# Three edits in a two-block layer kernel: one scaling with both norms between the blocks, the output projection's norm tile by tile, and whole gate products in the first twenty heads

## The chip, the cores and the metric

The kernel runs on one core of one Trainium2 chip. The metric is device microseconds of one execution; lower is better. A core has TensorE (PE in the profile, with PEld for its weight loads), VectorE (DVE), ScalarE (ACT), GpSimd (POOL) and SyncE (SP), which here only issues DMAs.

## The reference, cut to what matters

All data are float32, 1024 tokens of width 1024. Two blocks run one after the other: a first one with differential attention, a gated delta rule and 16 experts, then this:

```python
# end of the first block                      # start of the second
x3 = rms(x, final_g)                          # h = rms(x3, norm1_g_2);  proj = h @ w_in_2
...
# sparse attention: per row a top-256 of index scores, then 8 heads of width 64 over the chosen keys
# gates = 2048 columns of proj; y_ssm and y_att from the two branches
merged = sigmoid(g_ssm) * (y_ssm @ w_proj_ssm) + sigmoid(g_att) * (y_att @ w_proj_attn)
x4 = x3 + merged @ w_out_2
h2 = rms(x4, norm2_g_2)
out = x4 + (silu(h2 @ w_ffn_gate_2) * (h2 @ w_ffn_up_2)) @ w_ffn_down_2
```

`rms(x, g)` is x times the reciprocal root of the mean of its squares (plus 1e-6), times g. So between the blocks there are two norms one after the other on the same rows.

## The kernel before, in words

The program is a list of stages. Each stage is one block with an instruction list per engine; semaphores order the engines inside it, and at its end all engines meet (the profile shows that meeting as a wait for PEq). Tokens are cut in 8 tiles (TL) of 128 rows, t = 0 to 7; KD = 8 is the number of 128-wide pieces of the width.

**Experts** (`stage_experts`). PE multiplies 16 experts (L1820), whose weights of 12 MB each stream in over SP's queue. At the stage's start SP also loads small parameters of the second block and `final_g`, spread over the 128 partitions (L1777), ahead of the weights of expert 1. POOL gathers rows (L1796) and scatters results into `x_dram` (L1801).

**Between the blocks** (`stage_between`). SP loads the eight tiles of x (L1946), then w_in chunks (L1952). POOL makes xg = x * final_g (L1968). ACT takes the sum of squares of x (L1976) and of xg (L1980). For each pair of tiles, DVE runs seven tiny instructions (L2010 to L2016) which make both norms' reciprocals, ACT takes the roots (L1984), DVE scales twice: xn = xg * r1 * norm1_g (L2023) for the projection, and x3 = xg * r0 (L2027), which SP stores to DRAM (L1955). PE transposes xn (L2042); ACT (L1988) and DVE (L2005) each copy one half out of PSUM. SP then stores hT2 to DRAM (L1958).

**Sparse attention** (`stage_sparse`). 64 heads are written out in a fixed order, n = 0 to 63: eight for each token tile i, in the tile order 0, 1, 7, 6, 5, 4, 3, 2. A head of tile i works on (i + 1) * 128 keys. DVE does `attend(n)` (L2948: mask and row maximum), ACT the exponential (L2855), PE `values(n)`: transposes of the probabilities (L2821), `logits(n + 2)` (L2797), then a piece of a gate product (L2809), then the products with V (L2831) after ACT's copy of the transposes (L2863). ACT copies each finished gate product out (L2874) and SP stores it (L2779) and loads the next gate weights (L2776) into one of two buffers. In between, DVE runs 99 units of a bitwise search for the top-256 bounds (L2897 and small ones): 33 for each of three pairs of tiles (7 and 6, 5 and 4, 3 and 2), spread evenly over heads 0 to 15, 16 to 31 and 32 to 47; the last unit of each pair builds the masks and is long. Before the first head of the next tile can finish the last tile, DVE waits for all eight products (L2956).

There are 26 gate products here. Each is eight float32 matmuls of 512 columns, which the trace records as 16. The placement is one line:

```python
if n // 2 < GN:
    gates(n // 2, n % 2)
```

So head n carries half a product, and heads 0 to 51 carry all 26.

**Output projection** (`stage_out2`). PE multiplies the eight tiles (L3071, 16 float32 matmuls or 32 records each) into four pairs of PSUM banks; DVE adds x3 from DRAM (L3103); ACT sums squares (L3089). Only after the last tile come one root for all (L3091), DVE's scaling (L3112), PE's transposes (L3079) and ACT's copies (L3095). The next stage is `stage_ffn_up`, with PE's L3165.

Of the kernel before, what the change touches and what calls it, by code (L numbers as in the profile page):

```python
# [1736 lines left out]
def stage_experts(e):  # L1737
# [12 lines left out]
    e.fgain, e.s_fgain = A.take("final_gain", D), e.keep_sem("ex_fgain")  # L1750
# [10 lines left out]
    with nc.Block() as block:  # L1761
        @block.sync
        def _(sp):
# [13 lines left out]
            sp.dma_start(e.fgain, broadcast_rows(e.in_["final_g"])).then_inc(e.s_fgain, 16)  # L1777
# [14 lines left out]
        def _(pool):  # L1792
# [125 lines left out]
    A.give(*("w_" + n for n in names), "xe", "xT", "sg", "hid", "hidT", "y", "gcol", "rows", "idxT", "gateT")  # L1918
# [3 lines left out]
def stage_between(e):  # L1922
# [4 lines left out]
    e.x3_dram = nc.dram_tensor("x3_scratch", (L, D), F32).ap()  # L1927
    x = A.take("x", TL, D)
    gain = A.take("gain1", D)
    xg = A.take("xg", TL, D)  # L1930
# [3 lines left out]
    vv = A.take("vv", 2, TL)  # L1934
    s_x = [e.sem(f"bt_xin{i}") for i in range(TL)]
    e.w_p2, e.s_wp2 = A.take("w_p2", 3, KD, 512, high=True), [e.keep_sem(f"p2_w{i}") for i in range(3)]
    s_in, s_own, s_sq, s_sg, s_xg, s_var, s_rt, s_x3, s_n, s_tr, s_ev, s_ev2 = (
        e.sem(f"bt_{n}") for n in ("in", "own", "sq", "sg", "xg", "var", "rt", "x3", "n", "tr", "ev", "ev2"))
    e.s_hst = e.keep_sem("bt_hst")
    s_st = [e.sem(f"bt_st{i}") for i in range(TL)]  # L1940
    NP = TL // 2
    with nc.Block() as block:
        @block.sync
        def _(sp):
            for t in range(TL):
# [7 lines left out]
            for t in range(TL):  # L1953
                sp.wait_ge(s_x3, t + 1)
                sp.dma_start(e.x3_dram[t * P:(t + 1) * P, :], x[:, t]).then_inc(s_st[t], 16)  # L1955
            sp.wait_ge(s_ev, TL)
            sp.wait_ge(s_ev2, TL)
            sp.dma_start(e.hT_dram, e.hT2.rearrange("p a b -> p (a b)")).then_inc(e.s_hst, 16)  # L1958
            for t in range(TL):
                sp.wait_ge(s_st[t], 16)  # L1960

        @block.gpsimd
        def _(pool):
            for t in range(TL):
                if t == 0:
                    pool.wait_ge(e.s_fgain, 16)
                pool.wait_ge(s_x[t], 16)
                nc.gpsimd.tensor_tensor(xg[:, t], x[:, t], e.fgain, ALU.mult).then_inc(s_xg, 1)  # L1968

        @block.scalar  # L1970
        def _(act):
            def squares(t):
                act.wait_ge(s_x[t], 16)
                if t:
                    act.wait_ge(s_sq, t)
                nc.scalar.activation(junk[:, 0], x[:, t], ACT.Square, accum_out=ss[:, 0, t:t + 1]).then_inc(s_sq, 1)  # L1976
                act.wait_ge(s_xg, t + 1)
                if t:
                    act.wait_ge(s_sg, t)
                nc.scalar.activation(junk[:, 1], xg[:, t], ACT.Square, accum_out=ss[:, 1, t:t + 1]).then_inc(s_sg, 1)  # L1980

            def root(i):
                act.wait_ge(s_var, i + 1)
                nc.scalar.activation(vv[:, :, 2 * i:2 * i + 2], vv[:, :, 2 * i:2 * i + 2], ACT.Sqrt).then_inc(s_rt, 1)  # L1984

            def turned(t):
                act.wait_ge(s_tr, 2 * t + 1)
                nc.scalar.activation(e.hT2[:, 0:4, t * P:(t + 1) * P], ps[:, (2 * t) % 8, :].rearrange("p (a b) -> p a b", b=P), ACT.Copy).then_inc(s_ev, 1)  # L1988

            for i in range(NP):  # L1990
                squares(2 * i)
                squares(2 * i + 1)
                root(i)
                if i:
                    turned(2 * i - 2)
                    turned(2 * i - 1)
            turned(TL - 2)
            turned(TL - 1)

        @block.vector  # L2000
        def _(dve):
            step = Steps(dve, s_own)
            def turned(t):
                dve.wait_ge(s_tr, 2 * t + 2)
                nc.vector.tensor_copy(e.hT2[:, 4:8, t * P:(t + 1) * P], ps[:, (2 * t + 1) % 8, :].rearrange("p (a b) -> p a b", b=P)).then_inc(s_ev2, 1)  # L2005

            for i in range(NP):
                c = slice(2 * i, 2 * i + 2)
                dve.wait_ge(s_sg, 2 * i + 2)
                step(nc.vector.tensor_scalar(ss[:, :, c], ss[:, :, c], 1.0 / D, None, ALU.mult))  # L2010
# [1464 lines left out]
```

## Time and profile before

| | us |
|---|---|
| median of 3 runs | 3933.43 (3932.34 to 3933.57) |
| the profiled execution, its own time | 3939.54 |
| its span, first to last instruction | 3937.7 |
| PE busy in the span | 3623.9 |
| DVE busy | 1520.3 |
| ACT busy | 759.4 |
| POOL busy | 368.3 |

Times in the rows are microseconds from the span's start, unless marked ns. A timeline row is start, duration, engine, line, operation, output and input, and count; what stands in brackets is how long the engine had sat idle before it and what ended that. PEclk is the granted TensorE clock as a share of 2.4 GHz: 1.00 is that level, 0.50 is 1.2 GHz, a value between is a mean over time at both. The ends of matmuls are modelled, so the distance between starts says more than a matmul's duration.

### The profile page before, as it was taken

The numbers are of one execution on the slowest core, as the hardware profiler recorded it, in microseconds if no ns is written. First come the engines' busy times: TensorE is split into PE (matmuls) and PEld (weight loads), VectorE is DVE, ScalarE is ACT, GpSimd is POOL, SyncE is SP. The second block draws the span as 40 slices with busy tenths as digits, with TensorE's granted clock in tenths as the row PEclk, the third lists the DMA queues.
The fourth block names the chain that finished last, engine by engine and source line by source line (L and its number), as shares of the span: only waits on it lengthen the run. The fifth ranks groups of instructions, "written<-read, shape, count | busy, mean of one in ns | idle before, by whom it ended". The sixth has DMA issues, their size and how long they took to land. (4 is left out here: it accounts for less than half of the span.)

```text
span 3937.7 us, 32752 instructions
## 1 busy us (share of the span) xinstructions
PE 3623.9 (92%) x12692; PEld 1910.6 (49%) x12692; DVE 1520.3 (39%) x2703; ACT 759.4 (19%) x1408; POOL 368.3 (9%) x347
## 2 busy tenths in 40 slices
PE   7998999987889499999987999889999899999999
PEld 3445656544765344444433664345544444444444
DVE  3526662576333400001008563978521322222420
ACT  2004451442431000000002223223220111111000
POOL 0000000014620000000001020000000122221000
PEclk8999998988989699999988999889999999999999
DMA  6400000014332598888844032112132111110300
GB/s 241 142 9 23 1 1 14 30 58 120 87 124 96 176 347 311 316 318 322 309 154 186 0 64 83 51 30 75 33 112 96 43 43 43 43 50 30 144 22 32
DMA packets 200718, 431.22 MB, mean 110 GB/s; under 512 B 71561, under 2 KB 125993, under 8 KB 187761
## 3 DMA queue, kind: packets, MB, share of 16 engines
q1 hardware_dynamic: 191154, 397.85, 29.2%
q0 software_dynamic: 8272, 29.38, 2.5%
q8 instruction: 92, 1.51, 0.2%
q10 hardware_dynamic: 1152, 2.10, 0.1%
q14 instruction: 48, 0.39, 0.0%
HBM read 380.04 MB, written 48.07 MB: 109 GB/s over the span
## 5 line engine op out<-in xcount | busy, mean ns | idle before, releaser
L1820 PE MATMUL psum<-arena 128*128 128x512 f32 x1536 | 673.1, 596 | 5.5 <-DMA arena<-in_w_gate_dram 3.1
L3165 PE MATMUL psum<-arena 128*128 128x512 f32 x1232 | 531.5, 594 | 5.7 <-DVE arena L3223 4.1
L1820 PEld LDWEIGHTS psum<-arena 128*128 128x128 f32 x1536 | 290.4, 191 | 365.5 <-issue 362.5
L3165 PEld LDWEIGHTS psum<-arena 128*128 128x128 f32 x1232 | 234.4, 191 | 302.2 <-issue 294.5
L3319 PE MATMUL psum<-arena 128*128 128x512 f32 x528 | 228.6, 595 | 3.6 <-PEq L3138 3.6
L2809 PE MATMUL psum<-arena 128*128 128x512 f32 x416 | 201.7, 629 | 0.1
L742 PE MATMUL psum<-arena 128*128 128x512 f32 (+1 forms) x512 | 198.2, 543 | 1.1 <-PEq L456 1.1
L2897 DVE TENSOR_SCALAR_CACHE_REDUCE arena<-arena 128x1024 f32<-128x1024 f32 (+2 forms) x192 | 173.7, 943 | 1.9
L477 PE MATMUL psum<-arena 64*128 64x512 f32 (+1 forms) x384 | 156.1, 551 | 11.1 <-ACT arena L531 10.2
L3319 PEld LDWEIGHTS psum<-arena 128*128 128x128 f32 x528 | 100.3, 190 | 132.0 <-issue 131.8
L2113 PE MATMUL psum<-arena 128*128 128x512 f32 (+1 forms) x384 | 162.1, 582 | 0.0
L3234 DVE TENSOR_TENSOR arena<-arena,psum 128x512 f32<-128x512 f32 x44 | 30.3, 688 | 305.7 <-PE psum L3165 305.7
L742 PEld LDWEIGHTS psum<-arena 128*128 128x128 f32 x512 | 97.1, 191 | 96.3 <-issue 93.0
L1911 DVE SCALAR_TENSOR_TENSOR arena<-psum,arena 128x1024 f32<-128x1024 f32 x16 | 20.6, 1285 | 309.8 <-PE psum L1820 309.8
L3154 POOL TENSOR_TENSOR arena<-arena 128x512 f32<-128x512 f32 x22 | 28.7, 1304 | 1153.1 <-issue 783.3
L350 PE MATMUL psum<-arena 128*128 128x512 f32 (+1 forms) x320 | 127.8, 555 | 1.9 <-PEq L154 1.9
L2809 PEld LDWEIGHTS psum<-arena 128*128 128x128 f32 x416 | 77.9, 197 | 103.8 <-issue 102.3
L2113 PEld LDWEIGHTS psum<-arena 128*128 128x128 f32 x384 | 88.8, 233 | 68.5 <-issue 55.6
L1577 PE MATMUL psum<-arena 128*128 128x512 f32 x256 | 114.3, 607 | 1.8 <-PEq L1438 1.8
L1897 DVE TENSOR_TENSOR arena<-arena,psum 128x1024 f32<-128x1024 f32 x16 | 19.6, 1223 | 242.5 <-PE psum L1820 242.5
L3008 PE MATMUL psum<-arena 128*128 128x512 f32 x256 | 112.2, 601 | 0.9 <-PEq L2771 0.9
L3071 PE MATMUL psum<-arena 128*128 128x512 f32 x256 | 110.1, 592 | 2.4 <-PEq L2984 2.4
(514 smaller groups left out, 4674.2 us busy)
## 6 DMA issues: line engine op xcount, KB each, us to landing
arena<-in_w_gate_dram SPq DMA_DIRECT2D x32, 2048.0 KB, 7.4
arena<-in_w_up_dram SPq DMA_DIRECT2D x32, 2048.0 KB, 9.1
arena<-in_w_down_dram SPq DMA_DIRECT2D x32, 2048.0 KB, 8.0
arena<-in_w_mod_dram SPq DMA_DIRECT2D x12, 2048.0 KB, 9.5
arena<-gd_rows SPq DMA_DIRECT2D x56, 256.0 KB, 4.3
arena<-in_w_in_dram SPq DMA_DIRECT2D x22, 512.0 KB, 4.3
arena<-in_w_ffn_gate_dram SPq DMA_DIRECT2D x11, 1024.0 KB, 5.4
arena<-in_w_ffn_up_dram SPq DMA_DIRECT2D x11, 1024.0 KB, 5.4
```

The lines of the kernel that those rows point to most:

```text
L350: ins = nc.tensor.matmul(e.ps[:, i % 4, 0:n], w[:, c % 2, k, m * P:(m + 1) * P], e.hT[:, k, s:s + n], start=(k == 0), stop=(k == KD - 1))
L477: ins = nc.tensor.matmul(ps[:, 3 * m + j, 0:n], e.qT[64 * m:64 * m + 64, h, t * P:(t + 1) * P], e.kT[64 * m:64 * m + 64, h, c:c + n], star ...
L742: ins = nc.tensor.matmul(e.ps[:, i % 4, 0:n], w[:, (m // 2) % 2, k, (m % 2) * P:(m % 2 + 1) * P], e.hT[:, k, s:s + n], start=(k == 0), sto ...
L1577: ins = nc.tensor.matmul(ps[:, 2 * (t % 2) + j, :], cat(k)[:, t * P:(t + 1) * P], w[:, k, j * 512:(j + 1) * 512], start=(k == 0), stop=(k ...
L1820: ins = nc.tensor.matmul(ps[:, banks + j, :], lhs[:, k], W[n][:, h, k % 4, j * 512:(j + 1) * 512], start=(k == 0), stop=(k == KD - 1))
L2113: ins = nc.tensor.matmul(ps[:, BANK(i), 0:n], lhs, w[:, (c + 2) % 3, k, 0:n], start=(k == 0), stop=(k == KD - 1))
L2809: ins = nc.tensor.matmul(ps[:, 7, :], wg[:, c % 2, k], hT[:, k, n * 512:(n + 1) * 512], start=(k == 0), stop=(k == KD - 1))
L2897: nc.vector.tensor_scalar((rank, equal)[j][:, 0:(i + 1) * P], B(i), bound[:, j:j + 1], 0.0, ALU.is_ge, ALU.add, accum_out=count[:, j:j + 1 ...
L3008: ins = nc.tensor.matmul(ps[:, 2 * (i % 4) + g, :], wp[:, g, k, m * P:(m + 1) * P], y[:, k, n * 512:(n + 1) * 512], start=(k == 0), stop=( ...
L3071: ins = nc.tensor.matmul(ps[:, 2 * (t % 4) + j, :], e.merged[:, k, t * P:(t + 1) * P], w[:, k, j * 512:(j + 1) * 512], start=(k == 0), sto ...
L3165: ins = nc.tensor.matmul(out(q), left[:, k], right[:, k], start=first and k == 0, stop=last and k == 3, skip_group_check=not first)
L3319: ins = nc.tensor.matmul(ps[:, bank + t, :], left(c)[:, tok(t)], right(c), start=first and c == 0, stop=c == KC - 1, skip_group_check=not ...
```

## The change

1. **Between the blocks.** The POOL multiplication, x3 and its eight stores and the loading of `norm1_g_2` in this stage go. The experts' stage loads `final_g` and `norm1_g_2` into two free rows (`e.rows`), and POOL makes their product and the square of `final_g` there. In the stage itself ACT squares x once per tile and keeps the squares, DVE multiplies them by final_g squared and sums (`tensor_tensor_reduce`), and each tile is scaled once, by a factor with both norms. ACT does all sixteen copies out of PSUM. The first norm's factor is kept (`e.r3`).
2. **Output projection.** It loads x instead of x3 and makes x3 by one DVE instruction per tile. Root, scaling and transposes follow each tile: PE transposes tile t - 2 after it has multiplied tile t. The products use two pairs of PSUM banks instead of four.
3. **Gate products.** Heads 0 to 19 carry one whole product each, heads 20 to 31 a half each, and later heads none.

```diff
 stage_experts, SP:
-            sp.dma_start(e.fgain, broadcast_rows(e.in_["final_g"])).then_inc(e.s_fgain, 16)
+            sp.dma_start(e.rows[:, 1], broadcast_rows(e.in_["final_g"])).then_inc(s_fgain, 16)
+            sp.dma_start(e.rows[:, 2], broadcast_rows(e.in_["norm1_g_2"][0])).then_inc(s_fgain, 16)
 stage_experts, POOL, after gather(0) and gather(1):
+            pool.wait_ge(s_fgain, 32)
+            nc.gpsimd.tensor_tensor(e.rows[:, 2], e.rows[:, 2], e.rows[:, 1], ALU.mult).then_inc(e.s_gains, 1)
+            pool.wait_ge(e.s_gains, 1)
+            nc.gpsimd.tensor_tensor(e.rows[:, 1], e.rows[:, 1], e.rows[:, 1], ALU.mult).then_inc(e.s_gains, 1)
 stage_between, ACT:
+                nc.scalar.activation(x2[:, t % 4], x[:, t], ACT.Square, scale=D ** -0.5, accum_out=ss[:, 0, t:t + 1]).then_inc(s_sq, 1)
...
+            for t in range(4):
+                squares(t)
+            root(0)
+            squares(4)
+            turned(0)
+            turned(1)
+            root(1)
+            squares(5)
+            squares(6)
+            turned(2)
+            turned(3)
+            root(2)
+            squares(7)
+            turned(4)
+            turned(5)
+            root(3)
+            turned(6)
+            turned(7)
 stage_between, DVE:
+                nc.vector.tensor_tensor_reduce(out=junk[:, t % 2], in0=x2[:, t % 4], in1=gain_sq, scale=1.0, scalar=0.0, op0=ALU.mult, op1=ALU.add,
+                                               accum_out=ss[:, 1, t:t + 1]).then_inc(s_s1, 1)
...
+                nc.vector.scalar_tensor_tensor(out=xn[:, t % 2], in0=x[:, t], scalar=rr[:, 1, t:t + 1], in1=gains, op0=ALU.mult, op1=ALU.mult).then_inc(s_n, 1)
...
+            sum_with_gain(0)
+            sum_with_gain(1)
+            for i in range(TL // 2):
+                spread(i)
+                if i < TL // 2 - 1:
+                    sum_with_gain(2 * i + 2)
+                scaled(2 * i)
+                scaled(2 * i + 1)
+                if i < TL // 2 - 1:
+                    sum_with_gain(2 * i + 3)
 stage_sparse:
+    EARLY = 2 * HEADS + 4
+    halves = lambda n: ((n, 0), (n, 1)) if n < EARLY else (divmod(n + EARLY, 2),)
+    ready = lambda n: n if n < EARLY else (n + EARLY) // 2 if (n + EARLY) % 2 else None
...
-                if n // 2 < GN:
-                    gates(n // 2, n % 2)
+                for q, half in halves(n):
+                    if q < GN:
+                        gates(q, half)
...
-                if n >= 2 and n % 2 == 0 and n // 2 <= GN:
-                    gates((n - 2) // 2)
+                if n >= 1 and ready(n - 1) is not None and ready(n - 1) < GN:
+                    gates(ready(n - 1))
 stage_out2, PE:
+                ins.then_inc(s_mm, 1)
+                if t >= 2:
+                    turn(t - 2)
+            turn(TL - 2)
+            turn(TL - 1)
 stage_out2, ACT:
+            for t in range(TL):
+                squares(t)
+                root(t)
+                if t >= 2:
+                    turned(t - 2)
+            turned(TL - 2)
+            turned(TL - 1)
 stage_out2, DVE:
+                nc.vector.scalar_tensor_tensor(out=e.x4[:, t], in0=xr[:, t % 2], scalar=e.r3[:, t:t + 1], in1=g[:, 0], op0=ALU.mult, op1=ALU.mult).then_inc(s_x3, 1)
...
+            for t in range(TL):
+                residual(t)
+                spread(t)
+                modulated(t)
```

## Rows read from the trace of the kernel before

**Rows 1.** The page: busy time, share of the span and instructions of each engine.

```profile
PE 3623.9 (92%) x12692; PEld 1910.6 (49%) x12692; DVE 1520.3 (39%) x2703; ACT 759.4 (19%) x1408; POOL 368.3 (9%) x347
```

**Rows 2.** The timeline between the blocks, 2062 to 2112 us.

```profile
2066.34 18.47 POOL L1968 TENSOR_TENSOR arena<-arena 128x1024 f32<-128x1024 f32 x8 [11.35 <-DMA arena<-x_scratch]
...
2080.45 2.05 DVE L2016 TENSOR_TENSOR arena<-arena 128x2 f32<-128x2 f32 x1
...
2085.94 3.68 PE L2042 MATMUL psum<-arena 128*128 128x128 f32 x16 [34.74 <-DVE arena L2023]
...
2089.53 0.17 DVE L2016 TENSOR_TENSOR arena<-arena 128x2 f32<-128x2 f32 x1
...
2089.97 2.48 DVE L2023 SCALAR_TENSOR_TENSOR arena<-arena 128x1024 f32<-128x1024 f32 x2 [0.28 <-ACT arena L1984]
...
2111.12 1.30 PE L2142 MATMUL psum<-arena 128*128 128x128 f32 x8 [2.68 <-PEq L1942]
```

**Rows 3.** The timeline at the experts' start, around 1383 us.

```profile
1383.39 8.81 PE L1820 MATMUL psum<-arena 128*128 128x512 f32 x16 [3.09 <-DMA arena<-in_w_gate_dram]
```

**Rows 4.** The timeline at the end of the output projection, 3107 to 3125 us.

```profile
3107.13 1.22 DVE L3103 TENSOR_TENSOR arena<-arena,psum 128x1024 f32<-128x1024 f32 x1 [12.51 <-PE psum L3071]
3108.39 1.06 ACT L3089 ACTIVATE arena<-arena 128x1024 f32<-128x1024 f32 x1 [12.58 <-DVE arena L3103]
...
3118.40 0.86 PEld L3079 LDWEIGHTS psum<-arena 128*128 128x128 f32 x8 [0.34 <-DVE arena L3112]
...
3124.23 3.67 PE L3165 MATMUL psum<-arena 128*128 128x512 f32 x8 [0.99 <-PEq L3045]
```

**Rows 5.** DVE's timeline: `attend` of heads 0, 15, 16, 32, 47, 48, 53, 54, 55.

```profile
2466.96 0.29 DVE L2948 CUSTOM_DVE_ANT_0 arena<-psum,arena 128x128 f32<-128x128 f32 x1 [0.46 <-PE psum L2797]
...
2559.03 0.42 DVE L2948 CUSTOM_DVE_ANT_0 arena<-psum,arena 128x256 f32<-128x256 f32 x1
...
2580.08 1.22 DVE L2948 CUSTOM_DVE_ANT_0 arena<-psum,arena 128x1024 f32<-128x1024 f32 x1
...
2714.06 0.95 DVE L2948 CUSTOM_DVE_ANT_0 arena<-psum,arena 128x768 f32<-128x768 f32 x1
...
2809.98 0.83 DVE L2948 CUSTOM_DVE_ANT_0 arena<-psum,arena 128x640 f32<-128x640 f32 x1 [2.18 <-PE psum L2797]
...
2822.90 0.69 DVE L2948 CUSTOM_DVE_ANT_0 arena<-psum,arena 128x512 f32<-128x512 f32 x1
...
2847.97 0.69 DVE L2948 CUSTOM_DVE_ANT_0 arena<-psum,arena 128x512 f32<-128x512 f32 x1 [5.08 <-PE psum L2797]
2853.93 0.69 DVE L2948 CUSTOM_DVE_ANT_0 arena<-psum,arena 128x512 f32<-128x512 f32 x1 [5.08 <-PE psum L2797]
2856.46 0.69 DVE L2948 CUSTOM_DVE_ANT_0 arena<-psum,arena 128x512 f32<-128x512 f32 x1 [1.65 <-PE psum L2797]
```

**Rows 6.** PE's timeline: transposes of heads 6, 16, 20, 21; the next stage's first product.

```profile
2504.22 0.33 PE L2821 MATMUL psum<-arena 128*128 128x128 f32 x1 [1.42 <-ACT arena L2855]
...
2582.82 1.97 PE L2821 MATMUL psum<-arena 128*128 128x128 f32 x8 [16.06 <-ACT arena L2855]
...
2621.87 1.04 PE L2821 MATMUL psum<-arena 128*128 128x128 f32 x8
...
2630.02 1.04 PE L2821 MATMUL psum<-arena 128*128 128x128 f32 x8
...
2882.41 4.48 PE L3008 MATMUL psum<-arena 128*128 128x512 f32 x5 [0.94 <-PEq L2771]
```

**Rows 7.** Windows: busy us of PE, PEld, DVE, ACT, POOL, then PEclk, DMA share, GB/s.

```profile
2582.80:2593.10 10.30, 10.28 (x18) 4.82 (x19) 9.85 (x28) 2.73 (x4) 0.00 (x0) 0.50 0.28 76
...
2714.10:2822.90 108.80, 107.23 (x459) 63.30 (x458) 76.92 (x262) 32.35 (x58) 0.00 (x0) 1.00 0.19 59
...
2853.80:2876.00 22.20, 21.15 (x124) 14.15 (x123) 8.14 (x32) 11.38 (x30) 0.00 (x0) 1.00 0.00 1
```

**Rows 8.** The gate weights' loads (L2776) by source line.

```profile
DMA to landing us min/median/max: 4.0/4.2/5.4
```

More of the change, by code:

```diff
@@ L1917, in _ @@
                 output(i, False)
-    A.give(*("w_" + n for n in names), "xe", "xT", "sg", "hid", "hidT", "y", "gcol", "rows", "idxT", "gateT")
+    A.give(*("w_" + n for n in names), "xe", "xT", "sg", "hid", "hidT", "y", "gcol", "idxT", "gateT")
 def stage_between(e):
@@ L1926, in stage_between @@
     e.hT_dram = nc.dram_tensor("hT_scratch", (P, KD * L), F32).ap()
-    e.x3_dram = nc.dram_tensor("x3_scratch", (L, D), F32).ap()
     x = A.take("x", TL, D)
-    gain = A.take("gain1", D)
-    xg = A.take("xg", TL, D)
+    x2 = A.take("x2", 4, D)
     xn = A.take("xn", 2, D)
@@ L1973, in squares @@
                 act.wait_ge(s_x[t], 16)
[L1974 to L1980, printed above, removed]
+                if t >= 4:
+                    act.wait_ge(s_s1, t - 3)
+                nc.scalar.activation(x2[:, t % 4], x[:, t], ACT.Square, scale=D ** -0.5, accum_out=ss[:, 0, t:t + 1]).then_inc(s_sq, 1)
             def root(i):
                 act.wait_ge(s_var, i + 1)
-                nc.scalar.activation(vv[:, :, 2 * i:2 * i + 2], vv[:, :, 2 * i:2 * i + 2], ACT.Sqrt).then_inc(s_rt, 1)
+                nc.scalar.activation(rr[:, :, 2 * i:2 * i + 2], vv[:, :, 2 * i:2 * i + 2], ACT.Sqrt).then_inc(s_rt, 1)
             def turned(t):
[L1987 to L1998, printed above, removed]
+                for j in range(2):
+                    act.wait_ge(s_tr, 2 * t + j + 1)
+                    nc.scalar.activation(e.hT2[:, 4 * j:4 * j + 4, t * P:(t + 1) * P],
+                                         ps[:, (2 * t + j) % 8, :].rearrange("p (a b) -> p a b", b=P), ACT.Copy).then_inc(s_ev, 1)
+            for t in range(4):
[16 more added lines that the diff above has]
+            turned(7)
         @block.vector
@@ L2002, in _, with sum_with_gain, spread @@
             step = Steps(dve, s_own)
[L2003 to L2007, printed above, removed]
+            def sum_with_gain(t):
+                dve.wait_ge(s_sq, t + 1)
+                if t >= 2:
+                    dve.wait_ge(s_s1, t - 1)
+                nc.vector.tensor_tensor_reduce(out=junk[:, t % 2], in0=x2[:, t % 4], in1=gain_sq, scale=1.0, scalar=0.0, op0=ALU.mult, op1=ALU.add,
+                                               accum_out=ss[:, 1, t:t + 1]).then_inc(s_s1, 1)
+            def spread(i):
                 c = slice(2 * i, 2 * i + 2)
-                dve.wait_ge(s_sg, 2 * i + 2)
-                step(nc.vector.tensor_scalar(ss[:, :, c], ss[:, :, c], 1.0 / D, None, ALU.mult))
+                dve.wait_ge(s_s1, 2 * i + 2)
                 step(nc.vector.tensor_scalar(vv[:, 0, c], ss[:, 0, c], EPS, None, ALU.add))
@@ L2044, in _ @@
                         ins.then_inc(s_tr, 1)
-    A.give("x", "xn", "gain1", "final_gain", "junk", "ss", "xg", "vv")
+    A.give("x", "xn", "x2", "junk", "ss", "vv", "rows")
 TWO_PI = 2 * np.pi
@@ L3037, in stage_out2 @@
     xr = A.take("x_ring", 2, D)
-    g = A.take("gain", D)
+    g = A.take("gain", 2, D)
     h = A.take("h", 2, D)
@@ L3042, in stage_out2 @@
     s_x = [e.sem(f"o2_xin{i}") for i in range(2)]
-    s_g, s_mm, s_x4, s_sq, s_var, s_rt, s_own, s_h, s_tr, s_ev = (e.sem(f"o2_{n}") for n in ("g", "mm", "x4", "sq", "var", "rt", "own", "h", "tr", "ev"))
+    s_g = [e.sem(f"o2_g{i}") for i in range(2)]
+    s_mm, s_x3, s_x4, s_sq, s_var, s_rt, s_own, s_h, s_tr, s_ev = (e.sem(f"o2_{n}") for n in ("mm", "x3", "x4", "sq", "var", "rt", "own", "h", "tr", "ev"))
     two = lambda v: v.rearrange("p (a n) -> p a n", a=2)
```

117 lines of the change are left out of this document (49 added, 68 removed).

## The prediction

> **What bounds the kernel now.** I read the page first: PE is busy 92% of the span [rows 1], so only two things shorten the run: stretches in which PE waits, and PE work at the low clock. I then read the timeline of the three places that the change touches, and windows for the granted clock.
>
> Between the blocks PE sits 34.74 us without work before its first transposes [rows 2]. x starts to land at 2066.3; DVE's first tiny instructions, two elements per row, take up to 2.05 us while POOL multiplies (2066.34 to 2084.8), and 0.17 us once it is done [rows 2]. That convoy, not DMA, holds the stage from 2070 on.
>
> In the output projection PE works without a gap to about 3107.1, then the norm of all tiles runs alone: the next stage's PE starts at 3124.2 [rows 4], a tail of 17.1 us.
>
> In sparse attention the bound changes. Heads 0 to 15 go at DVE's pace, (2559.03 - 2466.96) / 15 = 6.14 us [rows 5], PE idle about 1.3 us in each [rows 6]; the mask unit of head 15 then holds everything from 2559.03 to 2580.08, and PE idles 16.06 us and comes back at 1.2 GHz: eight transposes take 1.97 us where they take 1.04 later [rows 6], and the window to 2593.1 is granted 0.50 [rows 7]. From head 20 on PE is the bound: 8.15 us a head [rows 6], and 107.2 of 108.8 us busy in heads 32 to 47, where DVE has 76.9 us of work [rows 7].
>
> **Part 1, experts.** One more broadcast row of 0.5 MB is in front of expert 1's weights on SP, and PE waits 3.09 us for these already [rows 3]. A load of 0.5 MB costs SP's queue between nothing and one such load; the bounds are 0 and 3 us, and I take 1.6. The two POOL multiplications (18.47 / 8 = 2.3 us each [rows 2]) delay the gather for expert 2, which is needed two experts' first halves later: nothing.
>
> **Part 2, between the blocks.** What is left on DVE: eight new reductions, eight scalings of 2.48 / 2 = 1.24 us, four groups of six tiny steps at 0.20 us from start to start, so 1.2 us each [rows 2]. The reduction is not in this stage's trace; the nearest row is the same kind of instruction in `attend`, 1.22 us for 1024 elements [rows 5], and its accumulator read makes 1.31. Bounds: 1.1 and, were both inputs in SBUF dearer, 1.6; I take 1.31. In order: x0 lands at 2066.2, ACT's square is done at 2067.4; two reductions to 2070.1; six steps to 2071.3. ACT has by then four squares (tiles land some 1.4 us apart) to 2071.7 and loads its root table until 2073.0, so the first scaling starts at 2073.25. From there DVE has 8 x 1.24 + 5 x 1.31 + 3 x 1.2 = 20.1 us, with 0.6 us of wait for the last root, to 2094.0. The last tile's eight transposes take 3.68 / 2 = 1.85 us at the low clock [rows 2], ACT's last copy 0.6: 2096.5. All copies now being ACT's costs nothing: 16 x 0.6 + 8 x 1.15 us of work in 30. The end meeting waits for the issue of SP's store of hT2, some 0.9 us: 2097.4 against 2111.1 [rows 2]. **-13.7**, with bounds -10 (dear reductions, late x) and -15. The x3 stores that go were hidden.
>
> **Part 3, output projection.** The transposes of tiles 0 to 4 go into the stream of products, 0.86 us each [rows 4]: +4.3. After the last product: the addition to +1.3, squares to +2.4 [rows 4], two small steps and a root (its table has been in since the first tile) to +3.2, the scaling to +4.5. ACT copies tiles 5, 6 and 7 in order and is through at +6.9; the next stage starts at +7.1 instead of +17.1. x3's instruction on DVE runs under the 13.7 us of a tile's products, and so does the wait for one of only two PSUM pairs. The last store of x4 leaves at +1.3 and the next stage needs it at +7. 4.3 + 7.1 - 17.1 = **-5.7**, bounds -3 and -7.
>
> **Part 4, gate products.** Half a product costs PE 5.96 - 2.53 = 3.43 us: heads 53 to 54 against 54 to 55 [rows 5]. The stage then goes in four stretches, each at the pace of the engine with more to do.
> - Heads 0 to 15: PE has 6.14 - 1.3 + 3.43 = 8.2 us a head, over DVE's 6.14; 16 x 8.2 = 131, plus 3.5 for some low clock at the start, from 2468: head 16 starts on PE at 2602. DVE arrives there too: `attend(15)` is ready two heads earlier and the mask unit takes 21.05 us [rows 5]. Before it was 2582.8 [rows 6]: +19.2, and the 16 us idle and the low clock after it are gone.
> - Heads 16 to 19: 8.15 + 3.43 = 11.6 us, four make 46.3; before 2621.87 - 2582.82 = 39.05 [rows 6]: +7.3, in all +26.5. Heads 20 to 31 carry a half as before: `attend(32)` at 2714.1 + 26.5 = 2740.6.
> - Heads 32 to 47, now without gates: PE needs 16 x 3.43 = 55 us less than 107, so DVE sets the pace. Its 76.9 us of work there [rows 7] are the lower bound; where it never waits, its instructions still take 10.30 us for 9.85 busy [rows 7], so 76.9 x 1.046 = 80.4, and I add 2 for the two tile changes: 82.4. `attend(48)` at 2823.0, as before. Here the 55 us that were bought for 26.5 bring only 26.4.
> - Heads 48 to 63: `values(48)` starts 1.75 us after its `attend`; six heads at 2.53 and one output (1.4) bring head 54 to 2841.3, and from its start to the next stage's first product is 25.1 us (PE 2857.3 to 2882.4 [rows 6]): 2866.4, -16.0.
> - The clock: PE idles some 9.6 us beside head 47's mask unit. After the idle time of before it ran 10.3 us at 1.2 GHz [rows 7], which costs half of that, 5.2; the work here is thinner, so I take 6, and 1 for dips in heads 32 to 47.
>
> Sum **-8.8**, bounds -15 (no clock loss) and +10. The loads of gate weights land after 4.2 us [rows 8] and now have one head of 8.2 us instead of two of 6: still hidden.
>
> **The sum.** 1.6 - 13.7 - 5.7 - 8.8 = -26.6. The profiled execution took 3939.5, so 3912.9; it stood 6.1 above the median of the runs, 3933.4, so the median goes to 3907.
>
> **Rivals.**
> *The gate edit gives nothing* (22%). If the clock costs 9 to 15 us more than I take, the 55 us of PE work taken out of heads 32 to 51 only pay for the 26.5 us put in ahead. For it: heads 32 to 47 leave PE at 53 of 82 us busy; idle PE lost the clock in rows 7. Against: no single gap in them reaches 2 us. Time: 3933.4 - 17.8 = 3915.6, up to 3922.
>
> *No gain to tell* (13%). The clock stays low in heads 48 to 63 after the idle time (some +20 more than I take), or the convoy between the blocks is replaced by a late x and dear reductions (+4). Time: 3925 to 3932.
>
> *Slower: the gate-free heads run at 1.2 GHz throughout* (5%). They hold no dense product any more. PE's 107.2 - 54.9 = 52.3 us in heads 32 to 47 double to 105, over DVE's 82.4, and heads 48 to 63 some 30 more. -26.6 + 22.6 + 30 - 7 = +19: 3952. It decides from 27 us of such loss on. Against it: heads 52 to 61 before, without gates too, were granted 1.00 through 22.2 us [rows 7].
> The Trainium skill (TensorE: Matmul & The Clock Gate, Part 4: PE-mode transpose) speaks for this rival: it says that transposes do not count as busy for the clock gate, and these heads are transposes and narrow products. By it the run would come out at about 3952; the window of gate-free heads at 1.00 does not agree, so its chance stays small.
>
> *All clean* (10%): no clock loss after head 47 and -15 between the blocks: 3898.
>
> **How the numbers follow.** My forecast has 50%, with its own range 3899 to 3915. What this measurement can tell from no change is 0.2%, 7.9 us: faster means under 3925.6, slower over 3941.3. Faster: 50 + 10 + 22 and a small part of the third case, 82%; same 12%; slower 6%. The range takes in the second case and leaves out half of the third and the fourth: 3893 to 3926.
>
> **What would show each step.** Between the blocks: PE's first transposes near 2075, the next stage near 2097, tiny DVE steps all at 0.17 us. Output projection: eight transposes after each of five tiles, a tail near 7 us. Sparse attention: heads 0 to 15 at 8.2 us with PE full, no gap at the first mask unit; DVE without waits in heads 32 to 47 and PE with gaps; `attend(48)` where it was; PEclk there and in the 20 us after it. The prediction falls if PEclk is 0.50 over the gate-free heads, if `attend(48)` comes over 10 us later than before, or if PE waits for gate weights in heads 0 to 5.

## The result

The changed kernel takes 3958.82 us (median of 6 runs, 3954.40 to 3962.63) against 3933.57 (median of 6, 3932.34 to 3938.04): a ratio of 1.0061, with a 95% interval of 1.0048 to 1.0074. It is slower by 25 us, where 27 us less was forecast. The rival that was given 5% forecast 3952.

The profiled execution took 3962.63 us, with a span of 3960.8, which is 23.1 over the span of before. The page, with the busy times and the granted clock in 40 slices:

```profile
PE 3685.2 (93%) x12692; PEld 1953.5 (49%) x12692; DVE 1519.8 (38%) x2721; ACT 755.9 (19%) x1407; POOL 354.1 (9%) x341
...
PEclk8998998998989699999989998998579999999999
```

PE has the same 12692 instructions as in [rows 1], and is busy 61 us longer. So nothing was added for it to do: it did some of it more slowly. PEclk shows where: a slice is 99 us long, and the 29th and 30th, from 2773 to 2971 us, have a 5 and a 7.

Stage by stage the two traces differ by this:

| | after minus before, us | predicted |
|---|---|---|
| experts' last product | +1.1 | +1.6 |
| from there to the next stage's first product (2097.64 against 2111.12) | -14.6 | -13.7 |
| to the first `attend` | -0.6 | 0 |
| sparse attention, first `attend` to the merge's first product (457.2 against 415.5) | +41.7 | -8.8 |
| merge | -0.5 | 0 |
| output projection (121.1 against 127.2) | -6.2 | -5.7 |
| the rest, all behind the output projection, and rounding | +2.2 | 0 |
| sum | +23.1 | -26.6 |

**Between the blocks.** The timeline of after, to be held against [rows 2]:

```profile
2075.50 3.67 PE L2041 MATMUL psum<-arena 128*128 128x128 f32 x16 [23.23 <-DVE arena L2020]
...
2082.48 1.22 DVE L2002 CUSTOM_DVE_ANT_0 arena<-arena 128x1024 f32<-128x1024 f32 x1
...
2089.87 0.17 DVE L2009 RECIPROCAL arena<-arena 128x2 f32<-128x2 f32 x1
...
2091.68 2.48 DVE L2020 SCALAR_TENSOR_TENSOR arena<-arena 128x1024 f32<-128x1024 f32 x2 [0.84 <-ACT arena L1967]
...
2097.64 1.94 PE L2142 MATMUL psum<-arena 128*128 128x128 f32 x8 [1.45 <-PEq L1945]
```

PE waits 23.23 us for its first transposes instead of 34.74, the tiny steps take 0.17 us now that POOL is silent, the new reduction takes 1.22, and the next stage starts at 2097.64.

**Output projection.** DVE and PE at its end, for [rows 4]:

```profile
3138.70 1.22 DVE L3127 TENSOR_TENSOR arena<-arena,psum 128x1024 f32<-128x1024 f32 x1 [9.07 <-PE psum L3086]
...
3145.19 2.71 PE L3200 MATMUL psum<-arena 128*128 128x512 f32 x3 [0.99 <-PEq L3050]
```

From the last product's addition to the next stage there are 6.5 us, where [rows 4] have 17.1.

**Sparse attention.** DVE's `attend` of heads 0, 16, 32, 38, 48, 54 and 55, for [rows 5], and PE's transposes of heads 16 and 20, for [rows 6]:

```profile
2452.84 0.29 DVE L2952 CUSTOM_DVE_ANT_0 arena<-psum,arena 128x128 f32<-128x128 f32 x1 [0.47 <-PE psum L2800]
...
2584.82 1.22 DVE L2952 CUSTOM_DVE_ANT_0 arena<-psum,arena 128x1024 f32<-128x1024 f32 x1
...
2730.07 0.95 DVE L2952 CUSTOM_DVE_ANT_0 arena<-psum,arena 128x768 f32<-128x768 f32 x1
...
2765.88 0.96 DVE L2952 CUSTOM_DVE_ANT_0 arena<-psum,arena 128x768 f32<-128x768 f32 x1 [2.42 <-PE psum L2800]
...
2836.46 0.68 DVE L2952 CUSTOM_DVE_ANT_0 arena<-psum,arena 128x512 f32<-128x512 f32 x1
...
2862.28 0.69 DVE L2952 CUSTOM_DVE_ANT_0 arena<-psum,arena 128x512 f32<-128x512 f32 x1 [3.87 <-PE psum L2800]
2867.04 0.69 DVE L2952 CUSTOM_DVE_ANT_0 arena<-psum,arena 128x512 f32<-128x512 f32 x1 [3.87 <-PE psum L2800]
```

```profile
2590.10 1.04 PE L2824 MATMUL psum<-arena 128*128 128x128 f32 x8
...
2637.86 1.04 PE L2824 MATMUL psum<-arena 128*128 128x128 f32 x8
```

| stretch | after | before | predicted after |
|---|---|---|---|
| `attend` 0 to PE's first transpose of head 16 | 137.3 | 115.9 | +19.2 (measured +21.4) |
| `attend` 0 to `attend` 16 | 132.0 | 113.1 | not forecast (measured +18.9) |
| `attend` 0 to 32 | 277.2 | 247.1 | +26.5 (measured +30.1) |
| `attend` 32 to 48 | 106.4 | 108.8 | 82.4 |
| `attend` 48 to the merge | 73.5 | 59.5 | 43.4, and some 6 of clock |

The price of the edit came out near the forecast; of what it was to bring, heads 32 to 47 gave 2.4 us of 26.4, and the heads behind them lost 14. In head 38 DVE now waits 2.42 us for PE's `logits`: in most of heads 35 to 46 PE still sets the pace, though it has half as much to do. The timelines of PE and of DVE around heads 32 and 33, and windows from there on, say why (columns of the windows as in [rows 7]):

```profile
2732.33 0.88 PE L2824 MATMUL psum<-arena 128*128 128x128 f32 x6
...
2734.62 1.55 PE L2835 MATMUL psum<-arena 128*128 128x64 f32 x12
2738.98 1.38 PE L2824 MATMUL psum<-arena 128*128 128x128 f32 x6 [2.80 <-ACT arena L2859]
```

```profile
2732.50 0.69 DVE L2960 TENSOR_TENSOR arena<-psum,arena 128x512 f32<-128x512 f32 x1 [1.18 <-PE psum L2835]
...
2736.71 0.96 DVE L2952 CUSTOM_DVE_ANT_0 arena<-psum,arena 128x768 f32<-128x768 f32 x1
```

```profile
2735.20:2738.60 3.40, 0.98 (x9) 0.84 (x8) 3.26 (x12) 0.70 (x1) 0.00 (x0) 1.00 0.00 0
2738.60:2742.00 3.40, 3.02 (x8) 1.81 (x9) 3.19 (x11) 1.14 (x3) 0.00 (x0) 0.59 0.00 0
...
2741.00:2780.00 39.00, 38.22 (x123) 26.70 (x121) 26.40 (x92) 10.46 (x19) 0.00 (x0) 0.50 0.00 1
2780.00:2836.00 56.00, 54.85 (x182) 39.47 (x182) 40.88 (x137) 13.73 (x26) 0.00 (x0) 0.50 0.00 0
2836.00:2910.00 74.00, 67.73 (x212) 43.17 (x211) 15.32 (x56) 21.12 (x52) 0.00 (x0) 0.50 0.00 1
```

The last gate product ends at 2730.7. Head 32 is the first of a tile: DVE waits for the last products of the old tile, puts its output out (2732.50), does its share of the search, and comes to `attend(33)` at 2736.71. PE has nothing to cover this any more and waits 2.80 us for head 33's exponential. Six transposes took 0.88 us before the wait and take 1.38 right after it: the granted clock has gone from 1.00 (2.4 GHz) to 0.50 (1.2 GHz). It stays there for some 174 us, to about 2914, inside the next stage, although PE is busy 98% of the time in the first two of these last windows and 92% in the third. It came back in the merge, amid its dense float32 products; a full PE had not brought it back.

### The profile page after: what moved, and what is told of

Its sections match the earlier page's. It is cut to its first block and busy times, and to the rows that moved or that the text cites. A ratio compares the mean times of both kernels' runs of the same rounds, so it can differ in the third digit from the quotient of the medians.

```text
span 3960.8 us, 32749 instructions
## 1 busy us (share of the span) xinstructions
PE 3685.2 (93%) x12692; PEld 1953.5 (49%) x12692; DVE 1519.8 (38%) x2721; ACT 755.9 (19%) x1407; POOL 354.1 (9%) x341
## 5 line engine op out<-in xcount | busy, mean ns | idle before, releaser
L1825 PE MATMUL psum<-arena 128*128 128x512 f32 x1536 | 668.0, 593 | 4.5 <-DMA arena<-in_w_gate_dram 2.1
L3200 PE MATMUL psum<-arena 128*128 128x512 f32 x1232 | 534.0, 596 | 4.3 <-DVE arena L3258 3.3
L1825 PEld LDWEIGHTS psum<-arena 128*128 128x128 f32 x1536 | 288.5, 190 | 361.3 <-issue 358.3
L3200 PEld LDWEIGHTS psum<-arena 128*128 128x128 f32 x1232 | 235.5, 191 | 302.2 <-issue 296.8
L3354 PE MATMUL psum<-arena 128*128 128x512 f32 x528 | 229.6, 597 | 3.6 <-PEq L3173 3.6
L2812 PE MATMUL psum<-arena 128*128 128x512 f32 x416 | 189.1, 605 | 0.4
L3354 PEld LDWEIGHTS psum<-arena 128*128 128x128 f32 x528 | 100.7, 191 | 132.5 <-issue 132.3
L742 PEld LDWEIGHTS psum<-arena 128*128 128x128 f32 x512 | 97.5, 192 | 97.5 <-issue 94.2
L2812 PEld LDWEIGHTS psum<-arena 128*128 128x128 f32 x416 | 76.9, 191 | 101.0 <-issue 100.7
L2113 PEld LDWEIGHTS psum<-arena 128*128 128x128 f32 x384 | 88.6, 233 | 68.1 <-issue 55.1
L2835 PEld LDWEIGHTS psum<-arena 128*128 128x128 f32 x576 | 99.7, 257 | 43.3 <-issue 32.8
L1577 PE MATMUL psum<-arena 128*128 128x512 f32 x256 | 113.7, 604 | 1.8 <-PEq L1438 1.8
L2800 PE MATMUL psum<-arena 64*128 64x512 f32 (+3 forms) x192 | 108.7, 689 | 5.0 <-PEq L2644 5.0
L3086 PE MATMUL psum<-arena 128*128 128x512 f32 x256 | 110.9, 592 | 2.4 <-PEq L2988 2.4
```

The lines of the kernel that those rows point to most:

```text
L742: ins = nc.tensor.matmul(e.ps[:, i % 4, 0:n], w[:, (m // 2) % 2, k, (m % 2) * P:(m % 2 + 1) * P], e.hT[:, k, s:s + n], start=(k == 0), sto ...
L1577: ins = nc.tensor.matmul(ps[:, 2 * (t % 2) + j, :], cat(k)[:, t * P:(t + 1) * P], w[:, k, j * 512:(j + 1) * 512], start=(k == 0), stop=(k ...
L1825: ins = nc.tensor.matmul(ps[:, banks + j, :], lhs[:, k], W[n][:, h, k % 4, j * 512:(j + 1) * 512], start=(k == 0), stop=(k == KD - 1))
L2113: ins = nc.tensor.matmul(ps[:, BANK(i), 0:n], lhs, w[:, (c + 2) % 3, k, 0:n], start=(k == 0), stop=(k == KD - 1))
L2800: ins = nc.tensor.matmul(ps[:, 2 * (n % 2) + c // 512, 0:w], e.hd[hh, h // 2, i * P:(i + 1) * P], e.hd[hh, KB, c:c + w], start=True, stop= ...
L2812: ins = nc.tensor.matmul(ps[:, 7, :], wg[:, c % 2, k], hT[:, k, n * 512:(n + 1) * 512], start=(k == 0), stop=(k == KD - 1))
```

## The experiments

Times are medians; every ratio is to the kernel before, run on the same chip beside the kernel in question (its medians there were 3936 to 3937). "Dense work" means the float32 products of 512 columns that the gates are made of; "thin work" is the rest of a head: transposes, `logits`, and products of 64 columns with V.

**1 and 2. The change cut in two.** `undo_gates` is the changed kernel with the old placement of gate products, `gates_only` the kernel before with the new one. Parts 1 to 4 are those of the prediction. PE's side of the edit:

```diff
 undo_gates, from the changed kernel:
-                for q, half in halves(n):
-                    if q < GN:
-                        gates(q, half)
+                if n // 2 < GN:
+                    gates(n // 2, n % 2)
```

> The change with the gate products placed as before (half a product in each of heads 0 to 51). Theory (the gate edit alone loses, by the clock): the other two parts keep their gains of 13.5 and 6.1 us less 1.1 at the experts, so 3933.5 - 18.5 = 3915. Rival (the three parts disturb each other, the gates only show it): over 3925, with PEclk under 0.95 somewhere in the sparse stage.

> The kernel before with the gate edit alone. Theory: the sparse stage takes 457 us instead of 415, PEclk 0.50 from some 10 us after the last gate product to the next stage; 3933.5 + 42 = 3975. Rival (the shift of the stage by the other parts makes the clock fall): between 3925 and 3945.

`undo_gates`: 3915.93 us, ratio 0.9947 (0.9935 to 0.9960). `gates_only`: 3979.40 us, ratio 1.0111 (1.0097 to 1.0126). Parts 1 to 3 save 21 us and Part 4 alone costs 43. In `gates_only` sparse attention takes 457 us as in the changed kernel and shows the same clock; in `undo_gates` it takes 414.4. The windows over heads 39 to 46 and the start of head 47, first of `gates_only`, then of `undo_gates`:

```profile
2780.00:2836.00 56.00, 54.86 (x183) 40.20 (x182) 37.82 (x136) 13.98 (x27) 0.00 (x0) 0.50 0.00 1
```

```profile
2734.00:2790.00 56.00, 55.22 (x233) 32.57 (x232) 34.69 (x123) 16.59 (x32) 0.00 (x0) 1.00 0.14 42
```

PE looks equally full in both, 98 and 99%; only the clock column tells them apart.

**3 and 4. The other two parts alone.** `between_only` has the edits of the experts and between the blocks on the kernel before (the output projection makes x3 from x, its norm at the end as before). `out2_only` has the norm tile by tile, and takes x3 from DRAM:

```diff
 between_only, output projection, from the changed kernel:
-                if t >= 2:
-                    turn(t - 2)
-            turn(TL - 2)
-            turn(TL - 1)
 out2_only, from the changed kernel:
-                sp.dma_start(xr[:, t % 2], e.x_dram[t * P:(t + 1) * P, :]).then_inc(s_x[t % 2], 16)
+                sp.dma_start(xr[:, t % 2], e.x3_dram[t * P:(t + 1) * P, :]).then_inc(s_x[t % 2], 16)
-                nc.vector.scalar_tensor_tensor(out=e.x4[:, t], in0=xr[:, t % 2], scalar=e.r3[:, t:t + 1], in1=g[:, 0], op0=ALU.mult, op1=ALU.mult).then_inc(s_x3, 1)
```

> The kernel before with the edit between the blocks alone (and its rows loaded in the experts' stage; the output projection makes x3 from x but keeps its norm at the end). Both theories: -13.5 + 1.1, so 3921; if x3's new instruction in the output projection were on the path, up to 3931.

> The kernel before with the output projection's norm tile by tile alone, x3 loaded from DRAM as before. Both theories: -6.1, so 3927.5. If part of the 6.1 is given back in the next stage, whose first products wait for sums on DVE and POOL in any case, 3930 to 3933.

`between_only`: 3918.78 us, 0.9959 (0.9946 to 0.9972), so 16 us less (11 to 21). `out2_only`: 3930.21 us, 0.9985 (0.9977 to 0.9994), so 6 us less (2 to 9); its output projection takes 121.1 us in the trace, as in the changed kernel. Both terms hold, each by itself. In `out2_only` the median fell 6 us, but at 3930.21 it lies in the case that its expectation had for a part given back in the next stage; that was not looked into.

**5 and 6. Dense work put back.** In heads 32 to 63, the changed kernel gets extra float32 matmuls of 512 columns, whose result nobody reads; `dense1` has one in each head, `dense4` four (as much as a half gate product):

```diff
+                    elif n >= 32:
+                        if n == 32:
+                            pe.wait_ge(s_gev, GN)
+                        for k in range(4):
+                            nc.tensor.matmul(ps[:, 7, :], wg[:, 0, k], hT[:, k, 0:512], start=(k == 0), stop=(k == 3))
```

> The change, with one extra float32 matmul of 512 columns (its result is not used) in each of heads 32 to 63, where the gate piece stood before. Thin-work theory (the clock falls because these heads hold no dense product): PEclk back to 1.00 or near it; heads 32 to 47 go at DVE's pace (82 us), heads 48 to 63 take 43 + 14 = 57, against 106 and 74 now: 3959 - 41 = 3918. If one matmul is too little, PEclk stays 0.50 and PE has 27 us more at half speed: 3990 to 4010. Placement rival (the whole products up front are the loss, whatever the clock): no gain, 3959 or more.

> The same with four extra matmuls in each of heads 32 to 63, as dense as the kernel before. Thin-work theory: PEclk 1.00, heads 32 to 47 at the pace of before (109 us), heads 48 to 63 with 55 us more work (98): 3959 - (180 - 207) = 3986. It serves to see the clock with the density of before; placement rival: PEclk no better than with one.

`dense4`: 3984.49 us, 1.0118 (1.0101 to 1.0135): the clock is 1.00 through all of heads 32 to 63, and `attend` 32 to 48 takes 108.9 us, as before, with all that extra work. `dense1`: 3944.77 us, 1.0018 (0.9979 to 1.0056), but its eight times go from 3919.04 to 3975.69, and the mean granted clock of an execution goes with them, from 0.951 to 0.937. It was expected at 3918. In the profiled one (3943.52) the clock fell at head 33 as in the changed kernel, behind a wait of 1.95 us, and came back in the middle of the heads:

```profile
2730.00:2795.00 65.00, 64.22 (x184) 42.02 (x183) 32.16 (x117) 13.49 (x24) 0.00 (x0) 0.50 0.00 1
2796.00:2829.00 33.00, 27.53 (x143) 18.12 (x142) 31.12 (x107) 10.99 (x20) 0.00 (x0) 1.00 0.00 1
```

It was lost again beside head 47's mask unit, where PE waits 8.75 us. By the mean clocks, one dense matmul in a head wins the clock back early in some executions and late or never in others (only one of the eight has a trace); four keep it. The second row shows something else: as soon as PE has its clock, DVE is busy 31.1 of 33 us and PE has time to spare. That is the state that the prediction took for all of heads 32 to 47.

**7. DVE's work taken away.** `no_search3` leaves out the bitwise search of the last pair of tiles but for two of its units, so DVE has far less work in heads 32 to 47:

```diff
-                    bit(g, 31 - u)
+                    if g < 2:
+                        bit(g, 31 - u)
```

> The change, leaving out 31 of the 33 units of the bitwise search for the third pair of tiles, some 51 us of DVE work in heads 32 to 47, so that PE need not wait for DVE there. Idle-gap theory (the clock falls since PE waits for DVE there): PEclk stays 1.00; heads 32 to 47 take PE's 52 us and the mask unit, heads 48 to 63 43: 3959 - 70 = 3889. Thin-work theory: PE has no gap and the clock falls all the same; PE's work doubled sets the pace, 3950 to 3959.

3950.46 us, 1.0027 (1.0017 to 1.0037). PE's timeline at head 33, and a window behind it:

```profile
2726.98 1.55 PE L2835 MATMUL psum<-arena 128*128 128x64 f32 x12
2729.61 0.87 PE L2824 MATMUL psum<-arena 128*128 128x128 f32 x6 [1.08 <-ACT arena L2859]
```

```profile
2740.00:2812.00 72.00, 71.22 (x233) 51.10 (x231) 12.09 (x35) 18.70 (x36) 0.00 (x0) 0.50 0.00 1
```

The tile change is quicker without the search, and PE waits only 1.08 us. The clock fell here too, and stayed low for 171 us, with PE busy 99% and DVE 17% in the 72 us shown. So neither a busy DVE nor PE's share of waiting keeps the clock down.

**8. Gate products beside both mask units.** `mask15` gives whole products to heads 12 to 15 alone, where PE idled in the kernel before, and halves to all other heads up to 47:

```diff
-    EARLY = 2 * HEADS + 4
-    halves = lambda n: ((n, 0), (n, 1)) if n < EARLY else (divmod(n + EARLY, 2),)
+    WHOLE = range(12, 16)
+    parts = [(q, h) for q in range(GN) for h in range(2)]
+    plan = {}
+    for n in range(len(heads)):
+        plan[n], parts = (parts[:2], parts[2:]) if n in WHOLE else (parts[:1], parts[1:])
+    halves = lambda n: plan[n]
```

> The change, with halves of gate products in every head as before except heads 12 to 15, which carry a whole one; the 26 products end at head 47. Thin-work theory: the 16 us in which PE idled beside the first mask unit hold two products, the clock isn't lost there, and the gate-free heads are only the last 16: 3915 - 8 to -14 if they keep 1.00 as heads 52 to 61 did, 3902 to 3908; if the clock falls in them, 3925. Placement rival: 3915 or slower.

3899.83 us, 0.9901 (0.9885 to 0.9918): by the medians 37 us less than before, of which 21 are Parts 1 to 3 (`undo_gates`). `attend` 0 to 16 takes 112.6 us, so the four extra halves cost nothing. They don't save the clock there, as the expectation had it: PE still waits 4.81 us beside head 15's mask unit and is granted 0.50 for some 10 us. From `attend(48)` to the merge there are 46.4 us, of which the first 4 are still PE's work for head 47, half a product among it. The windows beside head 47's mask unit and over the gate-free heads behind it, and PE at the first transposes of head 48, at the products with V of heads 62 and 63, and at the merge:

```profile
2784.80:2797.10 12.30, 12.30 (x50) 6.71 (x49) 11.64 (x31) 2.82 (x5) 0.00 (x0) 1.00 0.06 21
2802.00:2839.00 37.00, 34.28 (x194) 22.07 (x193) 12.64 (x49) 19.40 (x48) 0.00 (x0) 1.00 0.02 6
```

```profile
2801.19 0.61 PE L2828 MATMUL psum<-arena 128*128 128x128 f32 x4
...
2837.49 0.88 PE L2839 MATMUL psum<-arena 128*128 128x64 f32 x6 [0.58 <-ACT arena L2871]
...
2839.28 1.39 PE L2839 MATMUL psum<-arena 128*128 128x64 f32 x6 [0.58 <-ACT arena L2871]
...
2843.58 8.87 PE L3016 MATMUL psum<-arena 128*128 128x512 f32 x13 [0.95 <-PEq L2778]
```

Sixteen heads begin without a gate product, at 1.00: PE came to them from dense work, past a mask unit beside which it never waited. Fifteen of them keep it, over waits of up to 0.78 us. In head 63 the clock falls (the same six products take 0.88 us, then 1.39) and stays low for the last 4.3 us of the stage. The kernel before does the same: it falls 2.5 us before its merge, in what [rows 7] had not looked at, since their last window ends at 2876.0.

**9 to 11. What loses the clock and what gives it back.** `burst36` is the changed kernel with one more whole product, its result not used, in head 36. `early16` has whole products in heads 0 to 15 and halves in 16 to 35. `gap47` is `mask15` with whole products in heads 12 to 19, so that the last one ends in head 43, ahead of head 47's mask unit.

```diff
 burst36, from the changed kernel:
+                    elif n == 36 and half == 0:
+                        pe.wait_ge(s_gev, GN)
+                        for k in range(KD):
+                            nc.tensor.matmul(ps[:, 7, :], wg[:, 0, k], hT[:, k, 0:512], start=(k == 0), stop=(k == KD - 1))
 early16, from the changed kernel:
-    EARLY = 2 * HEADS + 4
+    EARLY = 2 * HEADS
 gap47, from mask15:
-    WHOLE = range(12, 16)
+    WHOLE = range(12, 20)
```

> The change, with one extra whole product (eight matmuls, result not used) in head 36, when the clock has been low for some 20 us. Gap theory (a wait of PE at head 32 loses the clock, thin work cannot win it back but can keep it): PEclk 1.00 again during or after the burst and through heads 37 to 46, lost again beside head 47's mask unit where PE waits some 8 us; heads 48 to 63 slow as before; 3959 + 10 - 20 = 3949. Density theory (thin work at DVE's pace does not even keep it): 0.50 again within some 10 us; 3959 to 3970.

> The change with whole products in heads 0 to 15 instead of 0 to 19; the halves then end with head 35, so that dense work lies beside the wait at head 32. Gap theory: PEclk 1.00 through heads 36 to 46 and lost at head 47: heads 32 to 47 some 95 us, 3959 - 13.7 - 6 = 3939. Density theory: 0.50 from about head 37 on; 3950.

> The version with whole products in heads 12 to 15, which took 3899.8, now with whole ones in heads 12 to 19, so that the gates end at head 43 and PE waits some 8 us beside head 47's mask unit. All that differs after it are four half products less beside the mask unit. Gap theory: PEclk 0.50 from there to the end of the heads, which then take 73 us instead of 43: 3900 + 25 = 3925 to 3932. If thin work regains the clock: 3900 to 3908.

`burst36`: 3956.29 us, 1.0049 (1.0031 to 1.0066). Its windows before the burst, from the burst's end to the next wait, and from head 41 on, and PE at head 41:

```profile
2735.00:2758.60 23.60, 22.82 (x73) 15.65 (x71) 16.87 (x60) 6.80 (x12) 0.00 (x0) 0.50 0.00 1
2769.00:2784.00 15.00, 14.39 (x93) 10.94 (x92) 8.85 (x30) 5.77 (x10) 0.00 (x0) 1.00 0.00 0
...
2789.00:2892.00 103.00, 98.92 (x308) 64.56 (x307) 46.02 (x155) 28.68 (x65) 0.00 (x0) 0.50 0.00 1
```

```profile
2786.48 1.33 PE L2824 MATMUL psum<-arena 128*128 128x128 f32 x5 [3.10 <-ACT arena L2863]
```

The burst gave the clock back 5.5 us after its start; heads 37 to 40 kept it without dense work; PE waited 3.10 us at head 41, behind the next tile change, and it was gone for 123 us. The expectation had it kept up to head 46 and 3949 us. The intervals of `burst36` and of the changed kernel overlap: the extra product paid for itself, and for no more.

`early16`: 3933.05 us, 0.9991 (0.9979 to 1.0002). Here heads 36 to 40 carry no gates and come at full clock from head 35; the same wait at head 41 ends it, where the expectation had head 47:

```profile
2737.00:2756.00 19.00, 18.48 (x120) 14.04 (x118) 13.95 (x50) 8.21 (x14) 0.00 (x0) 1.00 0.04 15
2763.50:2845.00 81.50, 78.19 (x247) 51.99 (x247) 40.86 (x135) 21.75 (x47) 0.00 (x0) 0.50 0.00 1
```

```profile
2758.57 1.33 PE L2824 MATMUL psum<-arena 128*128 128x128 f32 x5 [3.10 <-ACT arena L2859]
```

`gap47`: 3939.33 us, 1.0007 (0.9997 to 1.0016), 40 us more than `mask15` although it only moves products forward. Heads 44 to 47 keep 1.00 without gates until PE waits, for 9.15 us, beside the mask unit; the clock falls in that wait, and everything behind runs at 0.50:

```profile
2809.09 1.11 PE L2828 MATMUL psum<-arena 128*128 128x128 f32 x4 [9.15 <-ACT arena L2863]
```

```profile
2807.00:2870.00 63.00, 59.35 (x179) 37.18 (x180) 13.55 (x50) 18.44 (x45) 0.00 (x0) 0.50 0.00 1
```

From `attend(48)` to the merge it needs 73.5 us, the same as the changed kernel. From PE's first transposes of head 48 to the merge, the same work in both kernels, it needs 71.8 us where `mask15` needs 42.4.

**12. The products spread finer.** `spread` gives single matmuls to the heads instead of halves: 5 to each of heads 0 to 11, 8 to 12 to 15, 4 to 16 to 19, 3 or 4 to the others, 4 to 44 to 47, and none after.

```diff
+    share = [5] * 12 + [8] * 4 + [4] * 4 + [3, 3, 4, 4, 3, 4, 4, 3, 4, 4, 3, 4] + [3, 4, 3, 3, 4, 3, 4, 3, 4, 3, 4, 3, 4, 4, 4, 4]
...
-                for k in range(4 * half, 4 * half + 4):
-                    ins = nc.tensor.matmul(ps[:, 7, :], wg[:, c % 2, k], hT[:, k, n * 512:(n + 1) * 512], start=(k == 0), stop=(k == KD - 1))
+                ins = nc.tensor.matmul(ps[:, 7, :], wg[:, c % 2, k], hT[:, k, n * 512:(n + 1) * 512], start=(k == 0), stop=(k == KD - 1))
```

> Gate products cut into single matmuls: five in each of heads 0 to 11, eight in 12 to 15, four in 16 to 19, three or four in 20 to 43, four in 44 to 47, none later. PE's idle time of 1.3 us a head in heads 0 to 11 takes twelve matmuls of 0.86 us out of the heads where PE is the bound, and the waits at heads 16, 32 and 48 keep dense work beside them. 3900 - 10 = 3890; if the copies out of the one bank, now in the middle of a head, hold PE, 3895 to 3905.

3896.55 us, 0.9904 (0.9887 to 0.9920). Sparse attention takes 396.9 us in its trace, against 401.1 in `mask15`, but the two ratios are the same within their intervals. These two are the best versions: 1% under the kernel before and about 1.6% under the changed one, and 17 to 18 us under `undo_gates` by their ratios. Of the 10 us more that `spread` was expected to bring, 3 can be seen in the medians, which these runs can't tell from nothing.

## Why the prediction was wrong

**Right: Parts 1 to 3.** Experts +1.1 against +1.6; between the blocks -14.6 against -13.7; output projection -6.2 against -5.7. The convoy behind POOL's multiplications was what held the stage between the blocks, as read from [rows 2]: with them gone, the tiny steps take 0.17 us. The two parts keep their value alone (`between_only`, `out2_only`) and together (`undo_gates`, -21, where -17.8 were forecast).

**Near: the price of Part 4.** PE came to head 16 after 21.4 us more, for a forecast of 19.2, and to head 20 after 8.7 more, for 7.3: 30.1 in all against 26.5. The trace of after shows what the sum left out. Heads 14 and 15 take PE 9.6 us each, not 8.2, since their `logits` are already those of heads 16 and 17, over eight pieces. Heads 16 to 19 are 11.6 us each as forecast, and behind head 17 come the last tile's output transposes, 1.4 us. Of the 20 halves that the change adds to heads 0 to 19, the four of heads 12 to 15 were free, as `mask15` shows (112.6 us to `attend(16)`, 113.1 before); the other 16 are what the 30 us were paid for.

**The step that failed: the clock.** It reads "I take 6, and 1 for dips in heads 32 to 47". Behind `attend(48)` the stretch took 73.5 us, 30.1 over the 43.4 that the sum gave it at full clock, so the clock cost 24.1 more than was taken. In heads 32 to 47 it cost about 22, where 1 was taken. That figure is an estimate from rows, since no kernel ran all these heads without gates at full clock. The steps from one `attend` to the next where it was full or DVE set the pace are 6.64, 4.51 and 4.50 us (heads 32 to 34) and 12.93 (47) in the changed kernel, 4.64, 4.51, 4.53 and 6.92 (35, 38, 39, 40; 36 and 37 taken like 38) in `early16`, and 4.37 each (41 to 46) in `dense1`. Their sum is 84.4, against 106.4 measured; DVE's pace, forecast at 82.4, was 2 too low. So the clock makes up 45 of the 50.5 us by which this stage was missed.

The third rival had both stretches closely: 105 for heads 32 to 47 (106.4), and 30 on top of 43.4 after them (73.5). In the first this is in part luck: it took PE's work doubled throughout, and in heads 32 to 34 and 47 DVE set the pace as before. Its cause was also another, no dense work; the runs show no dense work and a wait.

Two readings of [rows 7] led there.
- Its last window, gate-free heads at 1.00, was held against that rival. The reading was true for the stretch that it covers, and the conclusion too wide. It showed that such heads keep a full clock that they enter with. It could not show what they do after a wait, since PE came to heads 52 to 61 from gate products. `mask15` (heads 48 to 62), `early16` (36 to 40), `burst36` (37 to 40) and `gap47` (44 to 47) show the same keeping, over 13 to 39 us. The clock fell in or within 1.4 us behind a wait each time: 3.10 us in `early16` and `burst36`, 9.15 in `gap47`, 2.80 in the changed kernel, 1.08 in `no_search3`. The prediction had said of heads 32 to 47 that "no single gap in them reaches 2 us"; the one at head 33 is 2.80.
- Its first window, 10.3 us at 0.50 after an idle time of 16 us, was taken as the length of such a loss. It was the length with gate products in the heads: they gave the clock back. Without them nothing did until the merge, 174 us in the changed kernel, 171 in `no_search3`, 123 in `early16` and, after its second loss, in `burst36`. So the clock lost beside head 47, costed at 6 us, costs 29, as `gap47` against `mask15` shows for the same work (71.8 against 42.4).

With the clock held the forecast behind `attend(48)` was right: 43.4 less the 1.75 to PE's start of head 48 are 41.7, and `mask15` takes 42.4, with 4.3 us at half clock at its end. (Its 46.4 from `attend(48)` hold the dense work of head 47.) The prediction had put down the two tile changes of heads 32 to 47 as 2 us of DVE's time; their waits are where the clock went. That DVE would set the pace of gate-free heads at full clock is borne out as far as `dense1`'s second window and the steps above go. Its terms for this stage, -16.0, 6 and 1, make -9.0 and not -8.8, which changes nothing.

The Trainium skill (TensorE: Matmul & The Clock Gate, Part 4: PE-mode transpose) says that transposes do not count as busy for the clock gate in the way that other work does. This trace agrees as far as it goes: heads of transposes and narrow products did not win the clock back at 98% busy. By it alone, gate-free heads should also not have kept it, and they did.

**What stays open.** Which of the thin instructions fail to win the clock back was not separated: the transposes, the products of 64 columns or the `logits` of 64 rows. Nor was what loses it. The length of one wait does not settle it: in `mask15` 0.78 us at head 50 did not, and two of 0.58 us in heads 62 and 63 came ahead of a loss. The last two heads have no `logits`, so it may be what PE does beside the wait; no run tests that. In `no_search3` the end of the gate products and the wait of 1.08 us lie together, so that run alone doesn't tell which of them did it. `gap47` against `mask15` moves four heads' gates along with the wait; that heads 44 to 47 kept the clock up to the wait speaks for the wait.

## What to carry to other kernels

Before dense matmuls are moved out of a stretch, look for the waits that PE will have in what remains. In this kernel thin work kept a full clock but did not win it back, so the first wait of 1 to 9 us was paid with half speed until the next dense work, however full PE looked. Put the dense work beside the waits (here the tile changes and the mask units of heads 15 and 47) and let it end only where no such wait follows. A window at full clock shows what holds with its way of entering; ask how the changed order enters it.

## What the hardware showed that was not expected

- PE busy 98 to 99% in the records and granted 1.2 GHz for 39, 56 and 72 us on end. The prediction had taken a busy PE for one that regains its clock.
- One product of eight float32 matmuls of 512 columns in head 36 brought back 2.4 GHz after 31 us without; with single ones, one in each head, the same kernel spread over 3919 to 3976 us, with mean granted clocks from 0.951 to 0.937.
- The tiny DVE steps of two elements per row that had taken up to 2.05 us beside POOL's multiplications [rows 2] take 0.16 to 0.17 us without them.
